# Expert rows of a two-layer PEER block: which v rows TensorE adds up and which VectorE does

## The reference, cut to what matters

```python
def peer_ffn(h, w_q, sub_keys, u, v):
    q = (ht @ w_q).reshape(T, PEER_HEADS, 2, PEER_QDIM // 2)
    s = jnp.einsum('thpd,pnd->thpn', q, sub_keys).astype(jnp.float32)
    top_s, top_i = lax.top_k(s, PEER_TOPK)                    # the key search
    ...
    def chunk(args):
        xc, ec, gc = args
        act = jax.nn.gelu(jnp.einsum('cd,ced->ce', xc, u[ec]))        # u rows: dot products
        return jnp.einsum('ce,ced->cd', gc.astype(xc.dtype) * act, v[ec])   # v rows: weighted sum
```

## Time and profile before

| what | value |
|---|---|
| median of 3 runs | 2390.09 us (2385.39 to 2391.0) |
| the profiled execution, its own time | 2409.64 us |
| its span, first to last instruction | 2408.0 us |
| mean granted TensorE clock | 0.841 of full |
| gathers in it | 1024, each 512 KB |
| v rows on TensorE / on VectorE | 262 / 250 |

### The profile page before, as it was taken

How to read it: one execution, slowest core, us unless ns; L and a number is a source line. 1 busy time by engine, 2 the same in 40 slices (tenths; PEclk the granted TensorE clock), 3 DMA queues, 4 the chain that set the end, 5 groups by cost and what they waited for, 6 DMA issues and landing times.

```text
span 2408.0 us, 23361 instructions
## 1 busy us (share of the span) xinstructions
PE 1723.7 (72%) x7278; PEld 1193.4 (50%) x7278; DVE 1549.6 (64%) x3430; ACT 384.9 (16%) x1016; POOL 1131.1 (47%) x1124
## 2 busy tenths in 40 slices
PE   8999999999995465776547668654766856355566
PEld 6787878888875132552344346224535622011112
DVE  3344326634167797679865858887495888866664
ACT  2015201000231122110102211110221101000001
POOL 1000002210003477577646766665476667776774
PEclk9999999999998777898868779677888978667768
DMA  9632349985448699999999999999999999999996
GB/s 328 213 106 88 114 130 368 377 304 173 139 133 326 237 346 367 364 409 386 346 390 378 361 368 409 365 353 385 360 346 380 409 344 361 403 352 366 370 385 250
DMA packets 212256, 757.95 MB, mean 315 GB/s; under 512 B 23084, under 2 KB 28472, under 8 KB 212024
## 3 DMA queue, kind: packets, MB, share of 16 engines
q0 software_dynamic: 161280, 587.27, 64.1%
q1 hardware_dynamic: 50440, 167.35, 19.8%
q10 hardware_dynamic: 432, 2.03, 0.2%
HBM read 755.50 MB, written 1.07 MB: 314 GB/s over the span
## 4 chain that ended last, share of the span: by engine, by line
PE 36%; DVE 21%; issue 15%; POOL 12%; DMA 9%; another core or an unknown queue 5%; ACT 1%; SPq 0%; DVEq 0%; ACTq 0%; POOLq 0%
PE psL L517 26%; POOL W L508 12%; DVE W L1098 8%; PE psO L517 5%; DVE Z L1013 4%; PE psT L517 3%; DMA W<-experts_v,crow 3%; DMA W<-experts_u,crow 3%; DMA wring<-weights 3%; PE psS L517 2%; DVE bias L1019 1%; DVE Z L1019 1%; DVE bias L1557 1%; DVE bias L1560 1%
## 5 line engine op out<-in xcount | busy, mean ns | idle before, releaser
L508 POOL DMA_INDIRECT W<-experts_u,crow x512 | 542.8, 1060 | 424.6 <-DVE crow L1016 191.9
L1098 DVE SCALAR_TENSOR_TENSOR W<-W,psL 128x1024 f32<-128x1024 f32 x512 | 605.7, 1217 | 137.0 <-DMA W<-experts_u,crow 114.9
L508 POOL DMA_INDIRECT W<-experts_v,crow x512 | 537.3, 1049 | 329.9 <-issue 151.3
L517 PE MATMUL psL<-W,con 128*128 128x512 f32 x604 | 354.6, 727 | 215.9 <-DMA W<-experts_v,crow 124.9
L517 PE MATMUL psL<-N,wring 128*128 128x256 f32 x1744 | 395.8, 388 | 13.2 <-DVE N L1013 6.1
L517 PEld LDWEIGHTS psL<-N,wring 128*128 128x128 f32 x1744 | 336.1, 194 | 67.7 <-issue 17.3
L1013 DVE SCALAR_TENSOR_TENSOR Z<-W,crow,Z 128x1024 f32<-128x1024 f32 x246 | 315.5, 1282 | 65.5 <-DMA W<-experts_v,crow 40.9
L517 PE MATMUL psL<-W,relrow 128*128 128x512 f32 x444 | 264.9, 736 | 104.5 <-DMA W<-experts_v,crow 58.7
L517 PEld LDWEIGHTS psL<-W,con 128*128 128x128 f32 x604 | 127.4, 228 | 411.7 <-issue 380.3
L490 POOL DMA_DIRECT2D W<-ada x96 | 50.9, 530 | 500.5 <-DVE W L1249 490.8
L517 PEld LDWEIGHTS psL<-W,relrow 128*128 128x128 f32 x444 | 95.0, 231 | 256.6 <-issue 245.6
(11 more groups left out here) (234 smaller groups left out, 1561.8 us busy)
## 6 DMA issues: line engine op xcount, KB each, us to landing
wring<-weights SPq DMA_DIRECT2D x311, 512.0 KB
W<-ada POOLq DMA_DIRECT2D x96, 512.0 KB, 6.9
W<-experts_u,crow POOLq DMA_INDIRECT x512
W<-experts_v,crow POOLq DMA_INDIRECT x512
W<-rel_rows SPq DMA_DIRECT2D x1, 1536.0 KB, 10.4
X<-x_dram ACTq DMA_DIRECT2D x1, 1024.0 KB, 5.6
W<-rel_rows SPq DMA_DIRECT2D x1, 768.0 KB, 5.0
crow<-c_row ACTq DMA_DIRECT2D x1, 512.0 KB, 7.3
```

Source lines behind the costliest of these rows:

```text
L508: pool.indirect_dma_start(W[:, slot * D:(slot + 1) * D], None, experts_u if kind == "u" else experts_v, bass.IndirectOffsetOnAxis(ap=idx[: ...
L517: return pe.matmul(o, l, r, start=first, stop=last)
L1098: dve.scalar_tensor_tensor(out=row, in0=row, scalar=1.0, in1=hps, op0=ALU.mult, op1=ALU.mult, accum_out=dots[:, col:col + 1]).then_inc(row ...
```

## The change

`on_pe` sends more v rows to TensorE: of the v rows 60 to 99 of each tile those with i % 4 == 1 as well, so that TensorE adds three of four there and every second one elsewhere. These are ten more rows per tile: i = 61, 65, 69, 73, 77, 81, 85, 89, 93, 97. The numbers 60 to 99 count v rows, not places: they stand at places 145 to 223 of tile 0, and at places 153 to 227 of tiles 1 to 3. All else follows from the tables: the slots, what each gather waits for, the diagonals and both engines' loops.

```diff
 def on_pe(t, i):
-    return i % 2 == 0 or t == 0 and i < EARLY_V
+    return i % 2 == 0 or t == 0 and i < EARLY_V or 60 <= i < 100 and i % 4 == 1
```

## The result

| | before | after | ratio, 95% interval |
|---|---|---|---|
| median, first comparison | 2390.55 us (2385.39 to 2393.77) | 2414.25 us (2408.22 to 2417.03) | 1.0098 [1.0071, 1.0125] |
| the profiled execution | 2409.64 us, span 2408.0 | 2415.59 us, span 2413.9 | |

Slower by 1.0%, 24 us, where I had forecast 2388 us and given 2371 to 2402. The profiled execution of the kernel before was 19 us above the median of its runs, that of the changed kernel 1 us above its own; so the two profiles are only 6 us apart, and what follows reads them by stretches.

A forecast was written before the change was run, and what follows sets the result against it. DMA engines were taken as nearly full, with VectorE possibly holding gathers in windows below 409 GB/s. Tile 1 gained 2.1 us, tile 2 lost 0.5, tiles 0 and 3 nothing: 2 us off the median, 2388 us, range 2371 to 2402.

The forecast's parts named there:

- the trade itself: Tiles 1 and 2 to place 207: TensorE stops replace VectorE waits, 2 us gained and 0.5 us lost; chance 0.38.
- the third rival: Tile 3: TensorE at its lower clock becomes the limit, 1 us behind in each of nine groups, 2399 us; chance 0.06.
- From 177 to 207 nothing stops it: Tile 1: GpSimd issues these 30 places at 1.33 us each without a stop, 40 us.
- At places 226 to 232 of tiles 1 to 3 TensorE's distance falls to 8 or 9: Eight places take 10.2 us, a row 5.5 to land and 3.75 at most to be added; cost nothing.
- I take **0: Tile 0: place 223 comes at 1113.3 to 1117.4 against 1116.47, no DMA rate to spare, so no gain or loss.
- The gain at 207: Tile 1: place 207 is issued at 1519.1 against 1521.19, 2 us gained (bounds 4.9 gained, 0.5 lost).
- The second, the slots as the limit: Stop before place 163 outlasts gathers in store, some 5 us lost in each of three tiles, 2405 us; chance 0.18.
- The first rival: VectorE was the limit: waits at places 223, 207 and 207 of tiles 0 to 2 won, 18.2 us, 2372 us; chance 0.30.
- The sentence on "Perfetto Trace Analysis": Whole kernel: go by memory rate, not occupancy; work taken off VectorE is worth nothing, 2390 us; chance 0.08.

The follow-up runs named there:

- slow gathers: Group of four comparisons in which the kernel before took 2386 to 2412 us; each chip showed one group only.
- with copies: The change plus 27 unused 512 KB DRAM-to-DRAM copies issued by ScalarE in rounds 23 to 31 of tiles 0 to 2: 2447.58 us, 1.0151 of the kernel before.
- with copies 2: The change plus the same 27 unused 512 KB copies, run in another comparison: 2428.49 us, 1.0191 of the kernel before.
- quick gathers: Group of three comparisons in which the kernel before took 2305 to 2306 us.
- again: The change unaltered, run a second time: 2306.78 us, 1.0002 of the kernel before.
- third: The change unaltered, run a third time: 2304.78 us, 0.9996 of the kernel before.
- fourth: The change unaltered, run a fourth time: 2305.37 us, 0.9999 of the kernel before.

## Why the prediction was wrong

**What held.** TensorE's slots stopped GpSimd where the prediction had them stop it. Counted from place 151, which came 2.8 us earlier than before, place 163 was forecast at 1452.5, 169 at 1463.4, 177 at 1476.3 (1455.3, 1466.2 and 1479.1, less 2.8), and they came at 1450.7, 1462.2 and 1474.5. In tile 2 place 177 was forecast at 1911.5 and came at 1911.26, with place 151 itself 3.2 us later than before. Place 207, counted from 151, came 0.5 us earlier in tile 1 (forecast 2) and 0.9 us later in tile 2 (forecast 0.5). So in tiles 1 and 2 of this pair the trade itself, ten us of stops for ten us of VectorE's waits, came out to within 1.5 us. How near it came is partly luck: in the two other pairs with slow gathers the same stretches are 1.2 to 9.1 us longer. Tile 3 took 361.8 us where it had taken 363.4, and TensorE's granted clock there was 0.85 where it had been 0.74 (the earlier trace rows and the last window rows), so the third rival was out, as it was with only tile 3 changed.

**Small misses.** There is also a stop of 4.70 us at place 157, where the prediction had begun to count at 163; the wait at 163 is 9.46 us instead of 13. "From 177 to 207 nothing stops it" was nearly so (1.16 us at 185, 2.33 at 201): 43.5 us, not 40.

**The steps that failed** are two terms that the sum put at nothing. It came to 2 us gained; the profiles show 15.6 us lost in tiles 0 to 2 (6.0 + 3.7 + 5.9), of which tile 0 has 6.0 and the stretches behind place 207 of tiles 1 and 2 have 9.1.

The first stands behind place 207. "At places 226 to 232 of tiles 1 to 3 TensorE's distance falls to 8 or 9 ..., so I put nothing on it": the sum compared how long a row takes to land and be added with how long eight gathers take, and left out what stands ahead of both, the weights that VectorE must have given for the row, by way of its diagonal. GpSimd cannot get past place 232 before VectorE has come to 218, 14 places back, and ScalarE and TensorE have acted on its weights. The waits at 232 are 7.15 and 9.04 us, and the stretch is 4.2 and 5.0 us longer.

The second is tile 0: "I take **0**". It counted TensorE's rounds up to place 177 and not the slots of the first changed rows. GpSimd stopped for 5.79 us at 149 and for 9.13 us at 155 (at 161 it had waited 4.00 us before, and waits 4.28 now), and from place 145 to 207 the gathers took 7.2 us longer, of which 1.2 us came back by 255. In the other two pairs with slow gathers it is 5.6 and 5.2 us.

How long the weights take goes with the group of the comparison. From the issue of place 218 to the weights that VectorE gives when it comes there, and the wait at 232 that followed, in tiles 1 and 2:

| | issue of 218 to weights, us | wait at 232, us |
|---|---|---|
| slow gathers (the first comparison, with copies, with copies 2) | 22.3, 24.1, 19.9, 20.5, 23.9, 17.8 | 7.15, 9.04, 2.90, 6.78, 7.30, 0.31 |
| quick gathers (again, third, fourth, tiles 0 to 2 only) | 18.0, 14.5, 16.9, 15.6, 18.1, 14.4, 18.1, 15.6 | 0.30, 0.30, 0.30, 0.59, 0.71, 0.36, 0.30, 0.65 |

GpSimd issues 14 gathers in some 18 to 20 us there (from 1533.53 to 1553.3 in tile 1). Where the weights come clearly sooner than that, place 232 doesn't wait. With slow gathers the gather of 232 waits in five of six cases, with quick gathers in none. The five are those in which VectorE, between its work on place 207 and these weights, had gaps that nothing in the profile ends (3.8 to 10.1 us); in the sixth, and in every quick case, it had none. That these gaps make the weights late is a reading of the timelines, and what makes the gaps isn't known. The short distances have a price with quick gathers too, at place 226 (9 places back): up to 5.4 us of waiting for TensorE in tile 1, in a stretch that is shorter than before all the same.

**The pace under it.** The gain at 207 was also carried to the end of the tile as if the gathers behind it could run at 1.33 us each. From 207 to 255 the kernel before took 70.0 / 48 = 1.46 us a gather, and in tile 3, where no search holds them, 186 / 127 = 1.46 in the first comparison and 164 / 127 = 1.29 with quick gathers. So with slow gathers there was, as far as these rates tell, nothing to win behind 207 by a lighter VectorE, only something to lose; with quick gathers the same stretch was 1.9 and 3.3 us shorter after the change, for all its waits. In tiles 1 and 2 of the first pair that is what parts the two groups: 9.4 to 10.2 us more beside the query weights in both, 7.4 to 10.0 us paid back up to place 207 in both, and then a further 2 to 3 us won with quick gathers and 4 to 5 us lost with slow gathers. The other two pairs with slow gathers lose 2 to 3 us behind 207 and the rest before it, and tile 0, from place 145 to 255, loses 5 us or more in all three and gains some 3 with quick gathers. The row to have seen was at hand. The windows of 362 and 340 GB/s were taken as held by VectorE because it was 92 to 95% busy, and measured against 409 GB/s, a rate that only gathers with weights beside them showed. Tile 3, with gathers alone and VectorE idle for two fifths of the time, ran at 360.

**The rivals.** The second, the slots as the limit "and nothing returned later because the windows behind it are held by something else than VectorE", named the mechanism and put it at 2405 us with a chance of 0.18. It had the sign right and its size, 15 us against 24, is short; but "nothing returned later" isn't what this pair shows, where 10.0 and 8.6 us came back between 177 and 207. It priced neither tile 0 by itself nor the end of the tile. By the profiles 15.6 us are lost in three tiles (tile 0 from place 145, the others from 151, all to 255); the rest of the 24 us is not in this pair of profiles, of which that of the kernel before is 19 us over its median. The first rival (2372 us, 0.30) needed gathers at 409 GB/s behind the stops; even in the comparisons that had them the change was level, not 0.8% faster, because the stops were not covered by rows in flight (9.4 and 10.2 us more from 151 to 177). The sentence on "Perfetto Trace Analysis" of the Trainium skill, section "Identifying the Most-Contended Engine", is borne out behind place 207: 7.5 us taken off VectorE's busy time there (67.97 to 60.46) gave nothing. What the rule needs is the right ceiling, here 360 GB/s for gathers alone and not 409. Between 177 and 207, at 409 GB/s in both kernels, work taken off VectorE shortened the stretch by 9 us, because the gathers' waits there were for slots, and because some of the other traffic had gone ahead.

**What stays open.** With slow gathers, the rows beside the query weights cost 1.6% alone and the rows behind them 0.1% (with an uncertainty of 0.5%, and only tried with copies), though one trace of the latter shows 6.4 and 6.9 us more at 207 to 255. So the stops are enough to cause a loss, which the runs show, while place 232 is seen in the timelines alone, and a run that had it without the stops lost nothing clear of noise. How the change's own 1% divides between them isn't settled. Nor is why four rows cost more than ten; less relief for the same stops is argued, from the stretch of tile 2 above, and wasn't tried by itself. A kernel with the weights of rows 96 to 111 given earlier wasn't tried either, nor four rows with quick gathers.

## What to carry to other kernels

When an engine gets rows from another, follow its ring of slots through every place where its distance shrinks, and at each ask for the last thing that the row itself waits for: here not its landing but the weights, two engines up the chain. Measure what a stretch could gain against a stretch of the same kind of traffic in which nothing waits, not against the highest rate of the trace. Start the count at the first place whose distance shrinks, in every tile, also in the one where the sum seems to be nothing. And a trade of an early stop for later relief, which looks even on paper, can come out even or as a loss from one comparison to the next: here the same change was some 1% slower in three comparisons with slow gathers (twice with copies) and level in three others.

The version that did best, six slots for TensorE in the changed stretch, is 0.1 to 0.3% faster than the kernel before with quick gathers and 0.9% slower with slow gathers. No version that was run is faster in both groups.

## What was not expected of the hardware

Gathers alone have two paces. Tile 3's places 128 to 255 ran at 360 to 372 GB/s with the DMA engines at 0.95 to 0.97 of the time, or at 401 to 409 at 1.02 to 1.03; the changed kernel itself had 369 in the one group and 405 to 407 in the other. Between 1000 us and the end VectorE has 53.0 us of gaps marked "issue" and 55.0 marked "remote" in the kernel before, 80.7 and 49.5 in the changed one, and none of either in the changed one with quick gathers. In the slow group GpSimd also shows waits that no engine of the core ends. In the waits of GpSimd after the change, in all, count and longest:

```profile
POOL W L508 <- PE psL L517: 159.3, 50, 18.5
POOL W L508 <- DVE W L1098: 127.9, 57, 26.5
POOL W L508 <- remote: 29.6, 13, 4.7
```

The third line is 14.6 us in 6 waits in the kernel before of the first comparison, and is missing from all profiles of the quick group. Direct transfers beside the gathers fill the gap (409 GB/s with query weights, 421 with copies), and 27 copies of 512 KB cost 0.4 and 1.0%, 9.8 and 25.7 us. So in the slow group it isn't the 16 engines together that are full when gathers run alone. Nor is it the gathers alone that are slow there, since VectorE stops in the middle of work that needs none of them. What slows them, and whether the gaps have the same cause, wasn't found. The Trainium skill, "DMA: Bandwidth & Descriptors", section "Latency and other measured facts", has two of the sixteen engines usually slower than the others for transfers that GpSimd issues, with a cause that it calls a guess; no view here shows the engines one by one, so that is left open.
